# Router stage of a two-layer encoder step: logits inside the output products, one spread on VectorE, identity products in TensorE's pauses

## Chip, core and metric

One core of one Trainium2 chip runs the whole program. The metric is device microseconds per execution. Before the change three runs gave 1261.56, 1264.34 and 1266.49 us, median 1264.34 us.

## What is computed

One inference step of an encoder trunk with two layers, for 512 prompt rows and 64 sample rows of width 1024. The kernel pads them to 640 rows, five tiles of 128 (tile 4 holds the sample rows). Cut to what the change touches:

```
h = x @ w_in                                   # q, k, v, u, gv
mixed = concat(rms_norm(attention(q,k,v)), rms_norm(gelu(u) * (tril(W) @ LN(gelu(gv)) + b))) @ w_o
x = layer_norm(ALPHA * x + mixed, ln1_g, ln1_b)
scores = sigmoid(x @ w_router); sel = scores + router_bias          # 16 experts in 4 groups
best group by the sum of its two best sel; the two best experts inside it; weights normalised
y = sum over the chosen experts e of weight * ((silu(x @ wg[e]) * (x @ wu[e])) @ wd[e])
x = layer_norm(ALPHA * x + y, ln2_g, ln2_b)
```

## The kernel before

Each engine has its own instruction stream, written out by hand and held together by semaphores; an engine runs its stream strictly in the order written. A loop over the layers encloses everything, so each place in the code runs twice.

**Rounds.** After the projections, TensorE goes through rounds t = 0 to 7. A round may hold the attention scores of tile t, the output product of tile t-3 (`output`), the transposition and use of the attention weights of tile t-1 (`weighted_values`), the transposition of the normalised mixer outputs of tile t-2 (`turn_mixed`, tiles `mt`), the transposition of finished rows (`turn_rows_out`, tiles `rt`), and the router's logits of tile t-4 (`expert_logits`). An output product has two halves, c = 0 into PSUM bank A and c = 1 into bank B, each of 8 steps m = 0 to 7 of three 128x512 matmuls (`product`, L1608): 24 matmuls a half. The logits are computed from the rows before layer norm, with the gain folded into the router's weights, so that they need only the transposed rows `x1_t` that ScalarE copies out of PSUM (`router_rows_out`, L805); a correction with column sums (`sums`) follows on VectorE. One tile's logits are 8 source matmuls of 16 columns, which the trace shows as 16 instructions (L1744).

**VectorE** adds each output half to x (`mixed_out`, L1163), takes row statistics, subtracts the mean times the gain (`centre`, L1170; in halves for the last tile, L1365) and multiplies by the reciprocal deviation and adds the shift (`spread`, L1176). After round 7 it turns logits into scores for tiles 0 to 3, picks their experts, and does the same for tile 4 at the end, to `pick` at L1405. TensorE then counts ranks (L1795, L1798), VectorE makes the lists `cur_src` of the first experts' rows, and GpSimd gathers these rows from `x1_dram` (L617). GpSimd then sends ten slot scatters (L637), before it gathers the rows of expert 2.

**The last tile.** Its spread is divided before the change: ScalarE multiplies (L860), after VectorE's `centred`; GpSimd adds the shift (L594), stores the rows (L596) and clears the tile `rows` (L599), which gathers fill.

**Experts.** Each of the 16 experts' weights comes in units of 1 MB, loaded by SyncE into a ring `raw` of four. ScalarE makes the high part `w_hi` (L392), VectorE the low part `w_lo` (L398, `split_lo`), TensorE multiplies three products per pair (L1831, L1854). A unit's place in the ring is free for the next load when its low part is done.

Of the kernel before, what the change touches and what calls it, by code (L numbers as in the profile page):

```python
# [27 lines left out]
P = 128  # L28
# [4 lines left out]
NT = 5  # L33
# [89 lines left out]
def build(nc, x_prompt, x_sample, cache_k, cache_v, w_in, sinks, gm_ln_g, gm_ln_b, gm_ws, gm_bs,  # L123
# [5 lines left out]
    with ctx:  # L129
# [3 lines left out]
        def sem(name):  # L133
            return ctx.enter_context(nc.semaphore(name))
# [167 lines left out]
        ln1_t_in, gained_done, logit_done = sem("ln1_t_in"), sem("gained_done"), sem("logit_done")  # L302
        tables_done, centred, w12_done = sem("tables_done"), sem("centred"), sem("w12_done")
        spread_done = sem("spread_done")
        score_done, pick_done, slot_done = sem("score_done"), sem("pick_done"), sem("slot_done")
# [224 lines left out]
        def _(pool):  # L530
# [24 lines left out]
            with pool.Fori(0, DEPTH) as l:  # L555
# [34 lines left out]
                for t in range(NT):  # L590
                    if t == NT - 1:
                        hold(spread_done, l + 1)
                        xt = x[:, t, :].rearrange("p (a c) -> p a c", a=2)
                        pool.tensor_tensor(xt, xt, ln1_shift, ALU.add).then_inc(x1_ready, 1)  # L594
                    hold(x1_ready, NT * l + t + 1)
                    pool.dma_start(x1_dram[t * P:(t + 1) * P, :], x[:, t, :]).then_inc(x1_out, 16)  # L596
                    if t == NT - 1:

                        pool.memset(rows[:, :, :], 0.0).then_inc(rows_zero, 1)  # L599
                    if t == 0:  # L600
# [100 lines left out]
        def _(act):  # L701
# [24 lines left out]
            with act.Fori(0, DEPTH) as l:  # L726
# [131 lines left out]
                scores_of(2, NT - 1, NT)  # L858
                act.wait_ge(centred, l + 1)
                act.activation(x[:, NT - 1, :], x[:, NT - 1, :], ACT.Copy, scale=rs[:, NT - 1:NT]).then_inc(spread_done, 1)  # L860
                act.activation(warm[:, 5:6], eps, ACT.Silu)
# [142 lines left out]
        def _(dve):  # L1004
# [49 lines left out]
            with dve.Fori(0, DEPTH) as l:  # L1054
# [178 lines left out]
                for t in range(NT + 2):  # L1233
# [4 lines left out]
                    if t == 0:  # L1238
                        for r in range(NT):
                            gmlp_out(r)  # L1240
                    if t >= 4:
                        logits_out(t - 4)
                    if t == NT + 1:
                        sums_out()
                    if t >= 2:
                        rms_norm(t - 2)
                    if t >= 3:
                        mixed_out(t - 3)
                    if t == NT + 1:
                        mixed_lo(t - 2)  # L1250
                    if 3 <= t < NT + 1:
                        layer_norm(t - 3)
# [30 lines left out]
                dve.tensor_tensor(neg_mean[:, 0:NB], mv[:, 0:NB, 0], rs[:, 0:NB], ALU.mult)  # L1283
                dve.tensor_tensor(tiles(logits[:, 0:NC]), tiles(raw_logits[:, 0:NC]), over_experts(rs[:, 0:NB]), ALU.mult)
                dve.drain()
                dve.tensor_tensor(tiles(spread_cols), over_tiles(col_sums[:, 0:NE]), over_experts(neg_mean[:, 0:NB]), ALU.mult)
                dve.drain()
                dve.tensor_tensor(logits[:, 0:NC], logits[:, 0:NC], spread_cols, ALU.subtract)
                dve.drain()
                dve.tensor_tensor(tiles(logits[:, 0:NC]), tiles(logits[:, 0:NC]), over_tiles(col_sums[:, NE:2 * NE]),  # L1290
                                  ALU.add).then_inc(logit_done, 1)
# [89 lines left out]
                dve.sem_inc(logit_done, 1)  # L1381
                centre_half(1).then_inc(centred, 1)

# [203 lines left out]
        def _(pe):  # L1587
# [12 lines left out]
            def product(name, col, units, n, last=None, a_hi=xt_hi, a_lo=xt_lo, then=None):  # L1600
# [45 lines left out]
            with pe.Fori(0, DEPTH) as l:  # L1646
# [69 lines left out]

                def output(t, then=None):
                    wait_read(pe, ("mt", t, 1), l)
                    for c in range(2):
                        if t == 0:  # L1720
                            wait_unit(pe, l, 9 + 2 * c)
                        wait_free(pe, ("wo", c, t), l)
                        product(("wo", c, t), 0, [(2 * c % RB, 0), ((2 * c + 1) % RB, 4)], HALF,
                                last=True if t == NT - 1 else None, a_hi=mt_hi, a_lo=mt_lo, then=then if c else None)

# [6 lines left out]

                def expert_logits(t, halves=(0, 1)):
                    name = ("logit", t)
                    if t == 0:
                        pe.wait_ge(gained_done, l + 1)
                        pe.sem_inc(held_pe, 1)
                    for h in halves:
                        wait_read(pe, ("rt", t, h), l)
                        if h == 0:  # L1740
                            pe.sem_inc(held_pe, 1)
                            wait_free(pe, name, l)
                        for k in range(4 * h, 4 * h + 4):
                            ins = pe.matmul(bank_of(name)[:, 0:NE], x1_t[:, k, :], gained[:, k, :],  # L1744
                                            start=(k == 0), stop=(k == KT_N - 1))
                    if halves[-1]:
                        done(ins, name)

# [10 lines left out]
                for t in range(NT + 3):  # L1759
# [4 lines left out]
                    if t == 0:  # L1764
# [48 lines left out]
                for e in range(2):  # L1813
                    indices((e,))


# [170 lines left out]
```

## Time and profile before

| | |
|---|---|
| median of 3 runs | 1264.34 us |
| the profiled execution | 1264.73 us |
| its span, first to last instruction | 1263.1 us |
| TensorE matmuls busy | 1066.4 us, 84% of the span |
| VectorE busy | 906.0 us, 72% |
| ScalarE busy | 703.6 us, 56% |
| GpSimd busy | 235.1 us, 19% |
| mean granted TensorE clock | 0.921 of full speed |

The shares are means over stages with different limits. The chain of work that ended last, followed back from the end, tells which engine a stage waits for; the timeline of one engine shows in brackets how long it stood idle before an instruction and what released it; the windows give the granted clock of a stretch (1.00 is 2.4 GHz, 0.50 is 1.2 GHz). All times of rows are microseconds from the span's start.

### The profile page before, as it was taken

What the parts mean: (1) busy time and instruction counts of PE and PEld (TensorE: products, weight loads), DVE (VectorE), ACT (ScalarE), POOL (GpSimd) and SP (SyncE); (2) the same over time, 40 slices, a digit from 0 to 9 for tenths busy, and PEclk for the clock granted to TensorE, in tenths of its full rate; (3) what the DMA queues carried; (4) which work ended last, traced back from release to release, by engine and by line L of the source; (5) the groups of instructions that cost most, each with busy time, mean ns of one, the idle gap of its engine ahead of it and who ended that gap; (6) DMA issues with size and microseconds to landing.
All of it is one profiled execution on the core that took longest, in us unless ns stands there. A gap on an engine that the chain in (4) does not pass through costs nothing.

```text
span 1263.1 us, 16601 instructions
## 1 busy us (share of the span) xinstructions
PE 1066.4 (84%) x5364; PEld 886.8 (70%) x5364; DVE 906.0 (72%) x1138; ACT 703.6 (56%) x859; POOL 235.1 (19%) x174
## 2 busy tenths in 40 slices
PE   4999799958799999999289988989499999999920
PEld 3887588747677777877169867877377877777820
DVE  2573865379688888887677648645878888788838
ACT  2413674265577777776423247533567777677720
POOL 3000000028112223110321000000642122221003
PEclk9999889978899999999589987999699999999975
DMA  9423100028899999999714202000599999999851
GB/s 292 139 81 100 67 35 25 17 70 273 298 363 359 375 354 356 377 361 332 285 42 155 87 15 84 26 34 17 161 344 362 365 355 379 367 355 366 325 195 59
DMA packets 115748, 273.26 MB, mean 216 GB/s; under 512 B 10144, under 2 KB 13184, under 8 KB 114528
## 3 DMA queue, kind: packets, MB, share of 16 engines
q1 hardware_dynamic: 98608, 227.36, 51.0%
q0 software_dynamic: 14464, 33.01, 7.5%
q10 hardware_dynamic: 2608, 12.06, 2.6%
q8 instruction: 33, 0.54, 0.2%
q14 instruction: 35, 0.29, 0.1%
HBM read 262.02 MB, written 25.22 MB: 227 GB/s over the span
## 4 chain that ended last, share of the span: by engine, by line
PE 42%; DMA 19%; DVE 14%; issue 12%; ACT 7%; DVEq 2%; POOL 1%; POOLq 1%; ACTq 1%; SPq 0%
DMA raw<-in_w_gate 16%; PE bankA L1608 10%; PE bankB L1608 8%; DVE w_lo L398 6%; ACT w_hi L392 4%; PE bankC L1608 4%; PE bankD L1608 3%; PE bankA L1831 3%; DVE xt_lo L413 3%; PE bankG L1677 2%; PE bankB L1831 2%; PE bankC L1854 2%; PE bankD L1854 2%; PE bankE L1597 2%; PE bankH L1744 1%
## 5 line engine op out<-in xcount | busy, mean ns | idle before, releaser
L398 DVE TENSOR_TENSOR w_lo<-raw,w_hi 128x2048 fp32r<-128x2048 f32 x216 | 487.5, 2269 | 110.0 <-ACT w_hi L392 108.9
L392 ACT ACTIVATE w_hi<-raw 128x2048 fp32r<-128x2048 f32 x216 | 410.1, 1902 | 226.3 <-DMA raw<-in_w_down 57.0
L1831 PE MATMUL bankA<-w_hi,xt_hi 128*128 128x512 f32 x256 | 104.7, 409 | 25.3 <-DVE xt_lo L413 24.7
L1831 PE MATMUL bankB<-w_hi,xt_hi 128*128 128x512 f32 x256 | 102.8, 402 | 0.0
L1831 PE MATMUL bankA<-w_hi,xt_lo 128*128 128x512 f32 x256 | 102.0, 398 | 0.0
L1831 PE MATMUL bankA<-w_lo,xt_hi 128*128 128x512 f32 x256 | 101.7, 397 | 0.0
L1831 PE MATMUL bankB<-w_hi,xt_lo 128*128 128x512 f32 x256 | 100.2, 391 | 0.0
L1831 PE MATMUL bankB<-w_lo,xt_hi 128*128 128x512 f32 x256 | 99.8, 390 | 0.0
L623 POOL DMA_INDIRECT y_rows<-expert_out,idx x32 | 55.6, 1737 | 213.9 <-ACT expert_out L888 205.3
L617 POOL DMA_INDIRECT rows<-x_rows,idx x24 | 48.0, 2000 | 248.3 <-PE bankF L1597 232.4
L1831 PEld LDWEIGHTS bankA<-w_hi,xt_hi 128*128 128x128 f32 x256 | 49.4, 193 | 45.8 <-issue 36.1
L408 ACT ACTIVATE xt_hi<-bankE 128x512 fp32r<-128x512 f32 x42 | 24.5, 584 | 66.5 <-PE bankE L1597 66.4
L1831 PEld LDWEIGHTS bankA<-w_hi,xt_lo 128*128 128x128 f32 x256 | 49.2, 192 | 10.7
L1854 PE MATMUL bankC<-w_hi,xt_hi 128*128 128x512 f32 x128 | 53.6, 418 | 3.3 <-DVE xt_lo L413 3.3
L1831 PEld LDWEIGHTS bankA<-w_lo,xt_hi 128*128 128x128 f32 x256 | 49.4, 193 | 9.7
L1831 PEld LDWEIGHTS bankB<-w_hi,xt_lo 128*128 128x128 f32 x256 | 48.0, 188 | 10.5
L1831 PEld LDWEIGHTS bankB<-w_lo,xt_hi 128*128 128x128 f32 x256 | 48.2, 188 | 9.2
L1831 PEld LDWEIGHTS bankB<-w_hi,xt_hi 128*128 128x128 f32 x256 | 48.1, 188 | 9.0
L413 DVE TENSOR_TENSOR xt_lo<-bankE,xt_hi 128x512 fp32r<-128x512 f32 x42 | 28.7, 684 | 33.6 <-ACT xt_hi L408 33.6
L1854 PE MATMUL bankC<-w_hi,xt_lo 128*128 128x512 f32 x128 | 51.0, 398 | 0.0
L1854 PE MATMUL bankC<-w_lo,xt_hi 128*128 128x512 f32 x128 | 50.8, 397 | 0.0
L1854 PE MATMUL bankD<-w_hi,xt_hi 128*128 128x512 f32 x128 | 50.6, 395 | 0.0
(357 smaller groups left out, 2501.1 us busy)
## 6 DMA issues: line engine op xcount, KB each, us to landing
raw<-in_w_gate SPq DMA_DIRECT2D x64, 1024.0 KB, 8.2
raw<-in_w_up SPq DMA_DIRECT2D x64, 1024.0 KB, 7.9
raw<-in_w_down SPq DMA_DIRECT2D x64, 1024.0 KB, 7.3
raw<-in_w_in SPq DMA_DIRECT2D x12, 1024.0 KB, 9.8
raw<-in_w_o SPq DMA_DIRECT2D x8, 1024.0 KB, 5.4
y_rows<-y_rows ACTq DMA_DIRECT2D x8, 1024.0 KB, 7.9
x_rows<-x POOLq DMA_DIRECT2D x10, 512.0 KB, 3.0
raw<-in_w_in SPq DMA_DIRECT2D x4, 512.0 KB, 8.4
```

Of the source, the lines that this page charges most:

```text
L392: act.activation(w_hi[:, s % RB, :, 0:n], raw[:, s % RB, :, 0:n], ACT.Copy).then_inc(hi_done, 1)
L398: dve.tensor_tensor(w_lo[:, s % RB, :, 0:n], raw[:, s % RB, :, 0:n], w_hi[:, s % RB, :, 0:n].bitcast(F32), ALU.subtract).then_inc(lo_done, 1)
L408: act.activation(dst, bank_of(name)[:, :].rearrange("p (k n) -> p k n", k=4), ACT.Copy).then_inc(s, 1)
L413: read(dve.tensor_tensor(lo, bank_of(name)[:, :].rearrange("p (k n) -> p k n", k=4), hi.bitcast(F32), ALU.subtract), name)
L617: pool.indirect_dma_start(out=rows[:, e % 2, :], out_offset=None, in_=x1_dram, in_offset=bass.IndirectOffsetOnAxis(ap=src.bitcast(U32), ax ...
L623: pool.indirect_dma_start(out=y2_dram, out_offset=bass.IndirectOffsetOnAxis(ap=idx[:, e, 0:1].bitcast(U32), axis=0), in_=expert_out[:, e % ...
L1597: ins = pe.transpose(bank_of(name)[:, k * P:(k + 1) * P], src, ident)
L1608: ins = pe.matmul(out, a[:, k, col:col + P], w[:, slot, j, 0:n], start=(m == 0 and a is a_hi and w is w_hi), stop=(m == len(steps) - 1 and ...
L1677: ins = pe.matmul(bank_of(("o", t))[:, h * 64:(h + 1) * 64], probs_t[:, j % 2, 2 * a + b, :], v[b], start=(b == (0 if t else 1)), stop=(b ...
L1744: ins = pe.matmul(bank_of(name)[:, 0:NE], x1_t[:, k, :], gained[:, k, :], start=(k == 0), stop=(k == KT_N - 1))
L1831: ins = pe.matmul(out, a[:, 4 * k + t, (c % 2) * P:(c % 2 + 1) * P], w[:, (s + k) % RB, t, :], start=(k == t == 0 and a is xt_hi and w is ...
L1854: ins = pe.matmul(bank_of(f"down{h}")[:, :], a[:, 2 * j + r, cols], w[:, (s + j) % RB, 2 * r + h, :], start=(j == r == 0 and a is xt_hi an ...
```

## The change

Three things are changed, in both layers.

First, `output` runs before the logits in a round, and `product` calls a function after each step m. In rounds 4 to 7 `beside_first` places two of a tile's eight logit matmuls after each of the steps 0 to 3 of half A. In round 7 `beside_last` places the transposition of the last tile's first half after step 3 of half B, as before, and four of its logit matmuls after steps 6 and 7. The matmul for `sums` moves behind the output product of round 6. VectorE's copies of logits move behind `rms_norm`, and tile 3 is spread before its logits are read.

Second, the last tile is spread by one instruction on VectorE, right behind its second `centre_half`. ScalarE's multiplication and GpSimd's addition go, with the semaphores `centred` and `spread_done`. ScalarE clears `rows` in place of GpSimd, when that spread is done.

Third, TensorE multiplies the identity by itself into bank A, 14 times behind the last logits and 10 times behind the lists of the first two experts (`idle_products`); nothing reads these products.

```diff
@@ GpSimd
                 for t in range(NT):
-                    if t == NT - 1:
-                        hold(spread_done, l + 1)
-                        xt = x[:, t, :].rearrange("p (a c) -> p a c", a=2)
-                        pool.tensor_tensor(xt, xt, ln1_shift, ALU.add).then_inc(x1_ready, 1)
                     hold(x1_ready, NT * l + t + 1)
                     pool.dma_start(x1_dram[t * P:(t + 1) * P, :], x[:, t, :]).then_inc(x1_out, 16)
-                    if t == NT - 1:
-                        pool.memset(rows[:, :, :], 0.0).then_inc(rows_zero, 1)
@@ ScalarE
                 scores_of(2, NT - 1, NT)
-                act.wait_ge(centred, l + 1)
-                act.activation(x[:, NT - 1, :], x[:, NT - 1, :], ACT.Copy, scale=rs[:, NT - 1:NT]).then_inc(spread_done, 1)
+                act.wait_ge(x1_ready, NT * l + NT)
+                act.activation(rows.rearrange("p a (b n) -> p (a b) n", n=P), ident.unsqueeze(1).to_broadcast([P, 2 * KT_N, P]),
+                               ACT.Copy, scale=0.0).then_inc(rows_zero, 1)
@@ VectorE, rounds
+                    if t >= 2:
+                        rms_norm(t - 2)
                     if t >= 4:
                         logits_out(t - 4)
-                    if t == NT + 1:
-                        sums_out()
-                    if t >= 2:
-                        rms_norm(t - 2)
...
                         mixed_lo(t - 2)
+                        sums_out()
@@ VectorE, tile 3
                 row_stats(NB - 1).then_inc(var1_done, 1)
-                logits_out(NB - 1)
...
-                dve.reciprocal(rs[:, NB - 1:NB], sd[:, NB - 1:NB])
-                dve.drain()
+                spread(NB - 1, ln1_shift).then_inc(x1_ready, 1)
                 dve.tensor_tensor(neg_mean[:, 0:NB], mv[:, 0:NB, 0], rs[:, 0:NB], ALU.mult)
...
+                logits_out(NB - 1)
...
-                xt = x[:, NB - 1, :].rearrange("p (a c) -> p a c", a=2)
-                dve.scalar_tensor_tensor(out=xt, in0=xt, scalar=rs[:, NB - 1:NB], in1=ln1_shift,
-                                         op0=ALU.mult, op1=ALU.add).then_inc(x1_ready, 1)
@@ VectorE, tile 4
-                centre_half(1).then_inc(centred, 1)
+                centre_half(1)
+                xt = x[:, r, :].rearrange("p (a c) -> p a c", a=2)
+                dve.drain()
+                dve.scalar_tensor_tensor(out=xt, in0=xt, scalar=rs[:, r:NT], in1=ln1_shift,
+                                         op0=ALU.mult, op1=ALU.add).then_inc(x1_ready, 1)
@@ TensorE
-                    if then is not None and m == 3:
-                        then()
+                    if then is not None:
+                        then(m)
...
+                def beside_first(t):
+                    def then(m):
+                        if m < 4:
+                            expert_logits(t, (2 * m, 2 * m + 1))
+                    return then
+                def beside_last(m):
+                    if m == 3:
+                        turn_rows_out(NT - 1, (0,))
+                    if m >= 6:
+                        expert_logits(NT - 1, (2 * m - 12, 2 * m - 11))
...
-                    if t >= 4:
-                        expert_logits(t - 4)
+                    if t >= 3:
+                        output(t - 3, beside_first(t - 4) if t >= 4 else None, beside_last if t == NT + 2 else None)
                     if t == NT + 1:
...
-                    if t >= 3:
-                        output(t - 3, (lambda: turn_rows_out(NT - 1, (0,))) if t == NT + 2 else None)
...
-                expert_logits(NT - 1, (0,))
                 turn_rows_out(NT - 1, (1,))
-                expert_logits(NT - 1, (1,))
+                expert_logits(NT - 1, range(4, KT_N))
+                def idle_products(n):
+                    wait_free(pe, "gate", l)
+                    for _ in range(n):
+                        pe.matmul(bank_of("gate")[:, 0:P], ident, ident, start=True, stop=True)
+                idle_products(14)
...
                 for e in range(2):
                     indices((e,))
+                idle_products(10)
```

Three places in the order of the instructions. Round 5 on TensorE, before and after: `mt_hi` and `mt_lo` are the transposed mixer outputs, `ws,x_t` are the logits. The first two rows are the end of the round before.

```order
L1597 MATMUL bankF<-ident,u 128x128 x4
L337 REGISTER_ALU
L1744 MATMUL bankH<-ws,x_t 128x16 x8
L341 REGISTER_ALU
L1608 MATMUL bankA<-w_hi,mt_hi 128x512
L1608 MATMUL bankA<-w_lo,mt_hi 128x512
L1608 MATMUL bankA<-w_hi,mt_lo 128x512
```

```order
L1589 MATMUL bankF<-ident,u 128x128 x4
L340 REGISTER_ALU
L1600 MATMUL bankA<-w_hi,mt_hi 128x512
L1600 MATMUL bankA<-w_lo,mt_hi 128x512
L1600 MATMUL bankA<-w_hi,mt_lo 128x512
L336 REGISTER_ALU
L1736 MATMUL bankH<-ws,x_t 128x16 x2
```

The logits, which stood ahead of half A in a block of eight, now follow its first three matmuls in pairs.

The end of the router on VectorE, before and after: `sel` is the first use of tile 4's scores.

```order
L1378 SCALAR_TENSOR_TENSOR small<-bankH,small,ws 128x16
L1365 SCALAR_TENSOR_TENSOR x<-x,small,table 128x512
L1385 TENSOR_TENSOR sel<-score,small 128x16
L1310 TENSOR_TENSOR work_wide<-sel 128x4x2
L1311 TENSOR_TENSOR work_wide<-sel 128x4x2
```

```order
L1366 SCALAR_TENSOR_TENSOR small<-bankH,small,ws 128x16
L1353 SCALAR_TENSOR_TENSOR x<-x,small,table 128x512
L1373 SCALAR_TENSOR_TENSOR x<-x,small,ln_shift 128x1024
L1377 TENSOR_TENSOR sel<-score,small 128x16
L1298 TENSOR_TENSOR work_wide<-sel 128x4x2
```

One instruction of 128x1024, the spread of tile 4, now stands ahead of `sel`.

GpSimd at the last stores of rows, before and after:

```order
L596 DMA x_rows<-x 128x1024
L533 REGISTER_ALU
L594 TENSOR_TENSOR x<-x,ln_shift 128x1024
L596 DMA x_rows<-x 128x1024
L599 MEMSET rows 128x2048
L611 DMA table<-in_ln_g 128x1024
```

```order
L591 DMA x_rows<-x 128x1024 x2
L603 DMA table<-in_ln_g 128x1024
L604 DMA table<-in_ln_b 128x1024
L532 REGISTER_ALU x2
L532 ISA
L609 DMA rows<-x_rows,cur_src 128x1024
```

The addition and the clearing are gone from GpSimd's queue; nothing but DMA issues is left in it there.

## Rows read from the trace of the kernel before

**Rows 1.** Chain that ended last, first layer: start, us, what

```profile
189.42 1.89 PE bankH L1744 x16
191.31 5.60 PE bankA L1608 x24
...
212.74 7.14 PE bankA L1608 x24
...
219.88 5.44 PE bankB L1608 x24
...
236.61 7.17 PE bankA L1608 x24
```

**Rows 2.** Timeline of TensorE: start, us, engine, line, operation [idle before it <-releaser]

```profile
233.76 1.95 PE L1744 MATMUL bankH<-ws,x_t 128*128 128x16 f32 x16 [1.45 <-ACT x_t L805]
...
236.45 0.60 PE L1608 MATMUL bankA<-w_hi,mt_hi 128*128 128x512 f32 x1
...
263.25 0.60 PE L1597 MATMUL bankC<-ident,x 128*128 128x128 f32 x4
...
263.93 0.39 PE L1608 MATMUL bankB<-w_lo,mt_hi 128*128 128x512 f32 x1
```

**Rows 3.** Windows: us, busy PE, PEld, DVE, ACT, POOL, granted clock, DMA, GB/s

```profile
209.20:212.60 3.40, 1.95 (x19) 1.82 (x17) 1.29 (x2) 3.26 (x9) 0.00 (x0) 1.00 0.38 154
...
212.60:219.00 6.40, 6.40 (x23) 5.19 (x23) 1.66 (x4) 0.16 (x1) 0.00 (x0) 0.73 0.01 3
...
592.00:595.00 3.00, 1.35 (x9) 0.94 (x8) 2.50 (x4) 1.26 (x3) 0.61 (x1) 1.00 0.65 192
```

**Rows 4.** Timeline of VectorE, first layer, rounds 5 to 7

```profile
210.17 0.68 DVE L413 TENSOR_TENSOR mt_lo<-bankF,mt_hi 128x512 fp32r<-128x512 f32 x1
...
233.14 0.68 DVE L413 TENSOR_TENSOR mt_lo<-bankF,mt_hi 128x512 fp32r<-128x512 f32 x1
...
266.65 0.69 DVE L1163 SCALAR_TENSOR_TENSOR x<-x,bankB 128x512 f32<-128x512 f32 x1 [0.74 <-PE bankB L1608]
```

**Rows 5.** Timeline of VectorE, first layer, a spread and the router's end

```profile
256.37 1.28 DVE L1293 SCALAR_TENSOR_TENSOR x<-x,small,ln_shift 128x1024 f32<-128x1024 f32 x1
...
271.13 0.17 DVE L1385 TENSOR_TENSOR sel<-score,small 128x16 f32<-128x16 f32 x1
...
272.72 2.22 DVE L1396 TENSOR_TENSOR in_group<-sel,r 128x16 f32<-128x16 f32 x1
...
275.82 2.08 DVE L1405 TENSOR_SCALAR pick<-last,consts 128x16 bf16<-128x16 f32 x1
```

**Rows 6.** Timeline of GpSimd (POOL), first layer, the last tile

```profile
272.57 2.34 POOL L594 TENSOR_TENSOR x<-x,ln_shift 128x1024 f32<-128x1024 f32 x1 [13.82 <-ACT x L860]
...
276.05 1.82 POOL L599 MEMSET rows<- 128x2048 f32 x1
```

**Rows 7.** Timeline of TensorE, first layer, small work and waits

```profile
138.83 1.16 PE L1708 MATMUL bankG<-gv,ws_t 128*128 128x128 f32 x8
...
268.80 1.06 PE L1744 MATMUL bankH<-ws,x_t 128*128 128x16 f32 x8 [0.69 <-ACT x_t L805]
...
277.96 0.26 PE L1795 MATMUL bankH<-pick,before_b 128*128 128x96 bf16 x1 [8.10 <-DVE pick L1405]
...
322.75 1.12 PE L1597 MATMUL bankE<-ident,rows 128*128 128x128 f32 x4 [7.25 <-DMA rows<-x_rows,cur_src]
```

**Rows 8.** Timeline of ScalarE, first layer, the first expert's rows

```profile
286.87 0.60 ACT L408 ACTIVATE xt_hi<-bankE 128x512 fp32r<-128x512 f32 x1 [3.50 <-PE bankE L1597]
```

**Rows 9.** Timeline of GpSimd, the seventh slot scatter of either layer

```profile
301.58 3.09 POOL L637 DMA_INDIRECT slot_rows<-ints,slots  x1 [0.30 <-issue]
...
916.01 0.98 POOL L637 DMA_INDIRECT slot_rows<-ints,slots  x1 [0.30 <-issue]
```

**Rows 10.** Timelines of VectorE and TensorE, second layer, expert waits

```profile
912.19 0.17 DVE L1420 TENSOR_REDUCE first_idx<-bankG 128x2 f32<-128x8 f32 x1 [0.61 <-PE bankG L1809]
...
932.34 0.66 PE L1597 MATMUL bankE<-ident,rows 128*128 128x128 f32 x4 [2.40 <-DMA rows<-x_rows,cur_src]
```

More of the change, by code:

```diff
@@ L302, in build @@
         ln1_t_in, gained_done, logit_done = sem("ln1_t_in"), sem("gained_done"), sem("logit_done")
-        tables_done, centred, w12_done = sem("tables_done"), sem("centred"), sem("w12_done")
-        spread_done = sem("spread_done")
+        tables_done, w12_done = sem("tables_done"), sem("w12_done")
         score_done, pick_done, slot_done = sem("score_done"), sem("pick_done"), sem("slot_done")
@@ L1280, in _ @@
                 dve.wait_ge(sd1_done, NT * l + NB)
-                dve.reciprocal(rs[:, NB - 1:NB], sd[:, NB - 1:NB])
+                spread(NB - 1, ln1_shift).then_inc(x1_ready, 1)
+                dve.tensor_tensor(neg_mean[:, 0:NB], mv[:, 0:NB, 0], rs[:, 0:NB], ALU.mult)
                 dve.drain()
-                dve.tensor_tensor(neg_mean[:, 0:NB], mv[:, 0:NB, 0], rs[:, 0:NB], ALU.mult)
+                dve.tensor_tensor(tiles(spread_cols), over_tiles(col_sums[:, 0:NE]), over_experts(neg_mean[:, 0:NB]), ALU.mult)
+                logits_out(NB - 1)
+                dve.drain()
+                dve.tensor_tensor(tiles(spread_cols), over_tiles(col_sums[:, NE:2 * NE]), tiles(spread_cols), ALU.subtract)
                 dve.tensor_tensor(tiles(logits[:, 0:NC]), tiles(raw_logits[:, 0:NC]), over_experts(rs[:, 0:NB]), ALU.mult)
                 dve.drain()
-                dve.tensor_tensor(tiles(spread_cols), over_tiles(col_sums[:, 0:NE]), over_experts(neg_mean[:, 0:NB]), ALU.mult)
-                dve.drain()
[L1288 to L1291, printed above, removed]
-                xt = x[:, NB - 1, :].rearrange("p (a c) -> p a c", a=2)
-                dve.scalar_tensor_tensor(out=xt, in0=xt, scalar=rs[:, NB - 1:NB], in1=ln1_shift,
-                                         op0=ALU.mult, op1=ALU.add).then_inc(x1_ready, 1)
+                dve.tensor_tensor(logits[:, 0:NC], logits[:, 0:NC], spread_cols, ALU.add).then_inc(logit_done, 1)
                 dve.wait_ge(tables_done, l + 1)
@@ L1381, in _ @@
                 dve.sem_inc(logit_done, 1)
-                centre_half(1).then_inc(centred, 1)
+                centre_half(1)
+                xt = x[:, r, :].rearrange("p (a c) -> p a c", a=2)
+                dve.drain()
+                dve.scalar_tensor_tensor(out=xt, in0=xt, scalar=rs[:, r:NT], in1=ln1_shift,
+                                         op0=ALU.mult, op1=ALU.add).then_inc(x1_ready, 1)
                 dve.wait_ge(score_done, 2 * l + 2)
@@ L1715, in turn_mixed, with output @@
                         turn(("mt", t, h), l, [v[:, t, k * P:(k + 1) * P] for k in range(4)])
-                def output(t, then=None):
+                def output(t, first=None, second=None):
                     wait_read(pe, ("mt", t, 1), l)
@@ L1723, in output @@
                         product(("wo", c, t), 0, [(2 * c % RB, 0), ((2 * c + 1) % RB, 4)], HALF,
-                                last=True if t == NT - 1 else None, a_hi=mt_hi, a_lo=mt_lo, then=then if c else None)
+                                last=True if t == NT - 1 else None, a_hi=mt_hi, a_lo=mt_lo, then=(first, second)[c])
                 def turn_rows_out(t, halves=(0, 1)):
@@ L1731, in turn_rows_out, with expert_logits @@
                         turn(("rt", t, h), l, [x[:, t, (4 * h + k) * P:(4 * h + k + 1) * P] for k in range(4)])
-                def expert_logits(t, halves=(0, 1)):
+                def expert_logits(t, ks):
                     name = ("logit", t)
[L1735 to L1740, printed above, removed]
+                    for k in ks:
+                        if k == 0:
+                            wait_read(pe, ("rt", t, 0), l)
                             pe.sem_inc(held_pe, 1)
                             wait_free(pe, name, l)
[L1743 to L1747, printed above, removed]
+                            pe.sem_inc(held_pe, 1)
+                            pe.wait_ge(gained_done, l + 1)
+                        if k == 4:
+                            wait_read(pe, ("rt", t, 1), l)
+                        ins = pe.matmul(bank_of(name)[:, 0:NE], x1_t[:, k, :], gained[:, k, :],
+                                        start=(k == 0), stop=(k == KT_N - 1))
+                        if k == KT_N - 1:
+                            done(ins, name)
+                def beside_first(t):
[8 more added lines that the diff above has]
+                        expert_logits(NT - 1, (2 * m - 12, 2 * m - 11))
                 pe.wait_ge(k_done, NT * (l + 1))
```

## Prediction

> **What bounds the kernel now.** I read first the chain of work that ended last. In the rounds it stays on TensorE [rows 1]: for each tile 16 logit matmuls, 24 products of half A, 24 of half B. The reader is to see that half A lasts 5.60 us in round 4 and 7.14 and 7.17 in rounds 5 and 6, for the same 24 products, while half B lasts 5.44. The first layer's rows are shown; the second's stand 614.5 us later, with the same lengths to a few hundredths where I speak of both.
>
> Next TensorE's timeline [rows 2] and the granted clock [rows 3]. In rounds 5 to 7 TensorE stands idle (1.45 us in round 6) for ScalarE's `x_t`, runs the logits, and only then begins half A. The clock is still 1.00 over that idle time and the logits, and 0.73 over the first 6.4 us of half A: about half of that stretch ran at 1.2 GHz. At 592.0, an idle time of 1.65 us of 3.0, with no logits behind it, leaves the clock at 1.00. So what precedes the fall is the idle time and the block of 16-column matmuls together, and idle time of that length alone does not bring it.
>
> Then VectorE. After half B of the last tile it is VectorE's chain, from 266.65 to `pick` at 277.9, that everything waits for: TensorE stands idle 8.10 us before the rank at 277.96 [rows 4, 7]. In that chain two instructions of 128x16 last 2.22 and 2.08 us, where their like lasts 0.17 [rows 5]. Each stands beside a GpSimd instruction and ends with it: the addition, 272.57 to 274.91, and the clearing, 276.05 to 277.87 [rows 6]. So I read both as VectorE shut out by GpSimd, 2.05 and 1.91 us a layer.
>
> Behind the rank TensorE waits 7.25 us for expert 2's rows in the first layer and 2.40 in the second [rows 7, 10]; from there the experts follow the weights' DMA.
>
> **The sum, by layer.** It is made against the profiled execution, 1264.73 us (a span of 1263.1 and 1.6 around it), which is 0.4 above the median of the runs.
>
> *Round 4, nothing.* No idle time and no low clock there: 1.89 of logits and 5.60 of half A before, the same matmuls mixed after.
>
> *Round 5, 1.24.* Half A needs `mt_lo`, whose last piece ends at 210.85 [rows 4]; it can start 0.15 later, and the chain counts a product 0.15 behind its start. From 211.15: half A at the full clock 5.60, the logits inside it 1.89, half B 5.44, end at 224.08. Before, it ended at 212.74 + 7.14 + 5.44 = 225.32 [rows 1]. The logits' own price inside half A no row shows. The nearest is the block of four transpositions inside half B: 0.68 from its start to the second product behind it, less one product's 0.23, is 0.45 [rows 2], 0.11 for each instruction, so no surcharge for the interruption. Four pairs are 16 instructions; at 0.45 for four that is 1.80, and I take 1.89. Bounds: 1.4, if each group's first weight load hides under a long product (one of four free), and 2.4, if the change of shape costs 0.15 a group. That is +0.5 or -0.5 a round.
>
> *Round 6, 1.93.* `mt_lo` ends at 233.82, half A counts from 234.12, and 5.60 + 1.89 + 5.44 and 0.24 for `sums`, now behind the product, end at 247.29; before, 236.61 + 7.17 + 5.44 = 249.22 [rows 1, 4].
>
> *Round 7, 0.1.* TensorE could gain here as in round 5, but VectorE, which adds half B, stood idle for it only 0.74 us [rows 4], and its row of work becomes longer ahead of that point by some 0.6, as tile 3's spread (1.28 in all, [rows 5]) now stands ahead of its logits. So VectorE becomes the bound: 0.74 less 0.6. Bounds 0.7 and -0.3.
>
> *The tail, 2.68.* The addition's and the clearing's locks go, 2.05 + 1.91; the spread comes onto VectorE's chain ahead of `sel`, 1.28 [rows 5]. ScalarE's clearing waits for that spread and is hidden if it ends before the first expert's rows are split: ScalarE has 3.50 us idle ahead of that [rows 8], and it loses a multiplication; the clearing by GpSimd took 1.82 [rows 6]. GpSimd's gathers wait for it, and stay behind VectorE's lists in any case. I price it at nothing, with 0.2 as the upper bound.
>
> The Trainium skill, "SBUF — State Buffer", section "SBUF: two separate sides", says that VectorE and GpSimd share a port pair under an exclusive lock, in which the loser is blocked wholly, and that VectorE with two SBUF inputs takes it only against a GpSimd operation that reads SBUF. The addition agrees with this. A clearing reads nothing, and L1405 has one tensor as input, so by the page it would be blocked only in a two-port mode; by the other reading the tail would gain 1.91 less.
>
> *The identity products, nothing on the path.* Eight f32 matmuls of 128 columns took 1.16 [rows 7]. The 28 behind the last logits (each product being two instructions) cost 4.1 us at the full clock and 8.1 at the low one; the logits end at 269.86, and the rank, moved up by 2.68, comes at 275.28: room 5.4. The 20 behind the lists cost 2.9 or 5.8; the room to the first rows is about 4.3. They are covered at the full clock, which half B leaves behind. What they can give: the first expert's products at the full clock. Yet TensorE there waits for GpSimd's gather in the first layer (7.25), so a quicker product buys only a longer wait; in the second VectorE waits 0.61 for TensorE behind it [rows 10], of which I count half, 0.3.
>
> Per layer 1.24 + 1.93 + 0.1 + 2.68 = 5.95, both 11.9, and 0.3: 12.2. 1264.73 - 12.2 = 1252.5, and 0.4 lower for the median: **1252.1**. The bounds of the logits' price (2 rounds, 2 layers, 0.5 each) and of round 7 give 1249 to 1255.
>
> **The rivals.**
>
> *The slot scatters, both ways.* GpSimd's ten slot scatters stand ahead of the gather of expert 2. The seventh took 3.09 us in the first layer and 0.98 in the second [rows 9], and so TensorE's wait is 7.25 or 2.40: a difference of 4.85 a layer. The router now comes some 6 us earlier against weight splits that follow a DMA stream, so either layer can fall either way. Both short: 1252.1 - 4.85 = 1247.2. Both long: 1256.9.
>
> The Trainium skill, same page and section, says that a VectorE operation in such a mode holds up the descriptors which GpSimd writes for its own DMAs. By that rule a scatter would be long beside a weight split and short without one; [rows 9] show that both lengths occur, and the time that each would give is the two figures above.
>
> *The clock falls all the same.* If the idle time alone brought it, halves A of rounds 5 to 7 would stay at about 7.15: 1.54 and 1.57 lost in rounds 5 and 6, and up to 1.3 in round 7, 4.4 a layer: 1252.1 + 8.8 = 1260.9. Against it stands the row at 592.0 [rows 3].
>
> *Slower.* The small matmuls, now spread over halves A of four rounds and the end of half B in round 7, keep the clock low in the products among which they stand. One product takes 0.43 at the low clock and 0.23 at the full one, so each costs 0.2; the change's 5.95 are eaten by 30 more low products in a layer. If 48 more ran low in each layer, 12 in each of the four rounds: 1252.1 + 19.2 = 1271.3. For it: the clock fell behind such matmuls. Against it: round 4, where 16 of them came without idle time, stayed at 5.60 [rows 1].
>
> *The identity products hold up the rank.* At the low clock they end at 277.96, 2.7 behind the earlier `pick`: 5.4 in both layers, 1257.5. Against it: half B leaves the full clock.
>
> *The locks are none.* If the clearing is not what stretches L1405, the tail gains 1.91 less: 1255.9; if neither is, 1252.1 + 7.9 = 1260.0. The ends that coincide in [rows 5] and [rows 6] speak against it.
>
> **How the numbers follow.** Forecast 0.55; scatters both short 0.14, both long 0.11; clock falls all the same 0.09; identity products late 0.05; locks are none 0.03; slower 0.03. The predicted time is the likeliest case's, 1252.1. The range, 1246.0 to 1259.5, takes in both scatter cases with a margin, the late identity products and the bounds of the unknown prices. What this kernel's measurement can tell from no change is 0.5%: below 1258.0 or above 1270.7. Faster: 0.55 + 0.14 + 0.11 and what of the last cases lies below 1258.0, 0.83. Slower 0.03. Within: 0.14, most of it the clock.
>
> **What would show it.** In the timeline of TensorE, halves A of rounds 5 and 6 should start some 1.6 and 2.5 us earlier against the `mt_lo` before them and last 7.5 us with the logits in them, with the granted clock at 1.00. On VectorE no instruction of 128x16 at L1396 and L1405 of before should last over 0.3; from the end of the last half B to `pick` should be some 2.7 shorter. TensorE's wait before expert 2's rows should be 7 and 2 us. Wrong it is, if the granted clock in rounds 4 to 7 is below 0.95, if the rank waits for an identity product, if L1405's like still lasts 2 us, or if the scatters take another pattern, which moves the time by 4.85 and shows in that wait alone.

## The result, and the profile after

Four runs of the changed kernel gave 1242.93 to 1251.14 us, median **1247.89**, beside 1265.41 for four runs of before: a ratio of 0.986 with a 95% interval of 0.982 to 0.991. Two longer comparisons on two chips, of twelve and of eleven runs (c1 and c3 below), gave 0.994 (0.991 to 0.997) and 0.9945 (0.991 to 0.998), that is 1254.4 against 1261.6 and 1254.0 against 1260.0. One execution of c3 (1866.5 us) and one of e9 (2186.0 us) lie far outside all others and are left out. The change makes the kernel faster, by some 0.5 to 1.4%. How much it gives is better read from the stages than from the first four runs.

The table measures each stretch on TensorE, in every layer of the traces at hand, us. A round is counted from the end of a half B to the end of the next.

| stretch | before, 2 traces | changed, 3 traces |
|---|---|---|
| round 5 | 22.97 22.99 21.39 23.01 | 24.77 24.79 26.41 23.19 26.35 21.60 |
| round 6 | 23.91 23.86 23.90 23.90 | 21.61 21.61 21.60 21.64 21.62 21.62 |
| round 7 | 17.38 17.36 17.37 17.37 | 16.60 16.60 16.60 16.63 16.60 16.60 |
| last half B to `pick` | 11.29 11.26 11.30 11.27 | 9.53 8.90 8.93 8.92 8.90 8.89 |
| rank to the start of the experts' last product | 322.3 318.1 321.1 313.6 | 315.4 315.9 319.1 319.1 317.4 319.0 |

From round 3's half B to the rank the mean is 97.8 before and 94.5 after: 3.3 us a layer, 6.6 in all. The experts' stretch (the last row) differs by 1.1 us between the two means, and by up to 8.7 within a column.

The chain that ended last, first layer of the changed kernel, rounds 5 and 6 (start, us, what; L1600 is a product, L1736 the logits):

```profile
209.33 0.96 PE bankA L1600 x3
210.29 0.35 PE bankH L1736 x4
...
212.19 1.47 PE bankA L1600 x3
213.66 0.67 PE bankH L1736 x4
...
234.10 0.95 PE bankA L1600 x3
235.06 0.35 PE bankH L1736 x4
...
237.70 0.79 PE bankA L1600 x3
238.49 0.35 PE bankH L1736 x4
```

Three products and a pair of logits take 0.79 + 0.35 in round 6 and 1.47 + 0.67 in round 5: twice as long, for the same work. The windows (us, busy PE, PEld, DVE, ACT, POOL, granted clock, DMA, GB/s) give the reason:

```profile
211.50:216.50 5.00, 5.00 (x20) 4.42 (x19) 1.37 (x3) 0.00 (x0) 0.00 (x0) 0.50 0.02 3
...
234.00:241.70 7.70, 7.60 (x41) 6.56 (x42) 1.80 (x5) 1.82 (x6) 0.00 (x0) 1.00 0.01 2
```

The clock is 0.50 in round 5, that is 1.2 GHz, and 1.00 in round 6. Half A of round 5, which ran 7.14 before without logits [rows 1], lasts 10.76 with them.

VectorE's timeline at the end of the first layer's router answers to [rows 5]:

```profile
269.18 1.28 DVE L1373 SCALAR_TENSOR_TENSOR x<-x,small,ln_shift 128x1024 f32<-128x1024 f32 x1
270.38 0.17 DVE L1377 TENSOR_TENSOR sel<-score,small 128x16 f32<-128x16 f32 x1
...
271.98 0.18 DVE L1388 TENSOR_TENSOR in_group<-sel,r 128x16 f32<-128x16 f32 x1
...
273.05 0.23 DVE L1397 TENSOR_SCALAR pick<-last,consts 128x16 bf16<-128x16 f32 x1
```

The two instructions that lasted 2.22 and 2.08 now last 0.18 and 0.23, and the spread stands ahead of them. TensorE's timeline around the identity products, first and second layer (idle time and its end in brackets), answers to [rows 7]:

```profile
266.07 1.89 PE L1736 MATMUL bankH<-ws,x_t 128*128 128x16 f32 x8 [0.69 <-ACT x_t L797]
267.79 5.67 PE L1797 MATMUL bankA<-ident 128*128 128x128 f32 x28
273.34 0.22 PE L1806 MATMUL bankH<-pick,before_b 128*128 128x96 bf16 x1
...
873.66 1.07 PE L1736 MATMUL bankH<-ws,x_t 128*128 128x16 f32 x8 [0.69 <-ACT x_t L797]
874.58 3.37 PE L1797 MATMUL bankA<-ident 128*128 128x128 f32 x28
880.30 0.26 PE L1806 MATMUL bankH<-pick,before_b 128*128 128x96 bf16 x1 [2.35 <-DVE pick L1397]
```

In the first layer the last logits ran at a granted clock of 0.50 and the 28 instructions at 0.57, and these end as `pick` does (273.28); in the second there are 2.35 us to spare. Waits for expert 2's rows were 4.73 and 5.82 us, where [rows 7, 10] have 7.25 and 2.40:

```profile
314.84 1.12 PE L1589 MATMUL bankE<-ident,rows 128*128 128x128 f32 x4 [4.73 <-DMA rows<-x_rows,cur_src]
...
922.84 1.11 PE L1589 MATMUL bankE<-ident,rows 128*128 128x128 f32 x4 [5.82 <-DMA rows<-x_rows,cur_src]
```

### The profile page after: what moved, and what is told of

Same layout as the page of the kernel before. It is cut to its first block, busy times and chain, and to the rows that moved or that the text cites. A ratio compares the mean times of both kernels' runs of the same rounds, so it can differ in the third digit from the quotient of the medians.

```text
span 1248.6 us, 16799 instructions
## 1 busy us (share of the span) xinstructions
PE 1069.0 (86%) x5460; PEld 892.1 (71%) x5460; DVE 901.2 (72%) x1140; ACT 706.8 (57%) x859; POOL 214.5 (17%) x170
## 4 chain that ended last, share of the span: by engine, by line
PE 44%; DMA 16%; DVE 13%; issue 13%; ACT 6%; DVEq 3%; POOL 3%; POOLq 1%; ACTq 0%; SPq 0%
DMA raw<-in_w_gate 12%; PE bankA L1600 9%; PE bankB L1600 7%; DVE w_lo L397 4%; PE bankC L1600 4%; PE bankA L1843 4%; PE bankB L1843 4%; PE bankD L1600 4%; ACT w_hi L391 3%; DVE xt_lo L412 2%; POOL slot_rows L629 2%; PE bankC L1866 2%; PE bankG L1669 2%; PE bankD L1866 2%; PE bankE L1589 2%
## 5 line engine op out<-in xcount | busy, mean ns | idle before, releaser
L615 POOL DMA_INDIRECT y_rows<-expert_out,idx x32 | 50.1, 1566 | 215.3 <-ACT expert_out L882 215.3
L609 POOL DMA_INDIRECT rows<-x_rows,idx x24 | 40.8, 1699 | 249.9 <-PE bankF L1589 232.9
L1600 PE MATMUL bankA<-w_hi,mt_hi 128*128 128x512 f32 x80 | 38.7, 483 | 14.2 <-DVE mt_lo L412 7.7
```

Of the source, the lines that this page charges most:

```text
L609: pool.indirect_dma_start(out=rows[:, e % 2, :], out_offset=None, in_=x1_dram, in_offset=bass.IndirectOffsetOnAxis(ap=src.bitcast(U32), ax ...
L615: pool.indirect_dma_start(out=y2_dram, out_offset=bass.IndirectOffsetOnAxis(ap=idx[:, e, 0:1].bitcast(U32), axis=0), in_=expert_out[:, e % ...
```

## The experiments

Ratios are against runs of before on the same chip, with 95% intervals. "To the rank" is the stretch from round 3's half B to the rank in the two layers of the trace: 98.2 and 98.1 before, 95.2 and 94.6 in the changed kernel's first trace. Of these runs, e1 to e4 ran on one chip, c1, c2, e5 and e6 on a second, e8 to e10 on a third and c3 on a fourth, so e1 to e4 are compared with c1 by their ratios.

**Both kernels again (c1, c2, c3).** No edit.

> The changed kernel as it is, on the chip of this call, as the yardstick for the others and for a second trace. Theory (the change is worth what the steps of the trace add up to, and round 5 keeps the low clock in most executions): from the end of round 3's half B to the rank 94.5 to 95.3 us in a layer whose round 5 falls to the low clock and 91.4 in one that does not, against 98.2 before; tail from the last half B to pick 8.9; time 1248 to 1252 where before has 1262 to 1265. Rival (half of the first trace's gain lay in the experts, 272 us from expert 2's rows to the last products where before had 276 and 277, and comes from the change): 272 again in both layers.

> The kernel before as it is, for a second trace. Theory (the length of the experts varies by execution, by DMA): from expert 2's rows to the last products below 275 in at least one layer; all steps up to the rank as in the first trace within 0.2 us, 98.1 to 98.3 from round 3's half B to the rank. Rival (before's experts are longer by themselves): 275.5 or more in both layers.

> The changed kernel a third time, since its first two comparisons with before differ (0.986 and 0.994). Theory (the change is worth its steps up to the rank, 6 to 8 us, and the experts' length varies by execution): ratio 0.992 to 0.996; from round 3's half B to the rank 93 to 96.5 us by how round 5 falls; from the rank to the last down product anywhere from 313 to 322. Rival (the first comparison is the rule): ratio 0.985 to 0.988, and 315 to 316 from the rank to the last down product in both layers.

c1: 1254.36, ratio 0.994 (0.991 to 0.997). c3: 1253.99, 0.9945 (0.991 to 0.998). c2, one run of before: 1255.4. The stages are in the table above. To the rank c1 took 96.2 and 93.1, c3 96.2 and 91.4. c1's theory allowed 94.5 to 95.3 or 91.4 and missed in both layers, since round 5 has more lengths than two; its time of 1248 to 1252 missed as well. From the first `down` product, right behind expert 2's rows, to the last product before had 275.9 and 277.2 in its first trace and 274.4 and 270.7 in c2; the changed kernel 272.3 and 271.7, then 277.8 and 278.6 in c1, 271.8 and 278.7 in c3. So the length of the experts belongs to the execution, and the rival falls. Of the 14.46 us between the first two traces' spans, 6.5 lay ahead of the ranks, 9.1 in the experts, and the rest took 1.2 back. The wait for expert 2's rows also varies, in the same code (c1, then c3, both layers):

```profile
315.80 1.12 PE L1589 MATMUL bankE<-ident,rows 128*128 128x128 f32 x4 [2.86 <-DMA rows<-x_rows,cur_src]
...
920.98 0.66 PE L1589 MATMUL bankE<-ident,rows 128*128 128x128 f32 x4 [1.92 <-DMA rows<-x_rows,cur_src]
```

```profile
318.21 1.11 PE L1589 MATMUL bankE<-ident,rows 128*128 128x128 f32 x4 [7.15 <-DMA rows<-x_rows,cur_src]
...
916.00 0.66 PE L1589 MATMUL bankE<-ident,rows 128*128 128x128 f32 x4 [2.63 <-DMA rows<-x_rows,cur_src]
```

The traces also tell which scatters are long. In VectorE's timeline of before, these are the weight splits at the two scatters of [rows 9], first and second layer:

```profile
301.54 2.28 DVE L398 TENSOR_TENSOR w_lo<-raw,w_hi 128x2048 fp32r<-128x2048 f32 x1
...
916.04 2.30 DVE L398 TENSOR_TENSOR w_lo<-raw,w_hi 128x2048 fp32r<-128x2048 f32 x1
```

The scatter of 3.09 us begins at 301.58, just inside a split, and ends at 304.67, 0.86 behind the split's end. The scatter of 0.98 us begins at 916.01, just ahead of one. Of the 280 scatters of all 14 traces, 215 begin inside a split and end 0.85 to 0.92 us behind its end; the other 65 begin outside one, or within its first 0.04 us, and last 0.98 to 1.15. So a scatter's length depends on where it falls against VectorE's splits. No run moves a split to test this.

c2 missed one point: one of its four halves A of rounds 5 and 6, round 5 in the first layer, lasted 5.55 us and not 7.14, behind the same idle time and the same block of logits; that layer took 96.6 to the rank.

**Identity products ahead of half A (e4, e9).** e4 fills the wait for `mt_lo` in rounds 5 to 7; e9 uses `{5: 6}` alone.

```diff
+                    if t in {5: 6, 6: 6, 7: 2}:
+                        wait_free(pe, ("wo", 0, t - 3), l)
+                        for _ in range({5: 6, 6: 6, 7: 2}[t]):
+                            pe.matmul(bank["A"][:, 0:P], ident, ident, start=True, stop=True)
                     if t >= 3:
                         output(t - 3, ...)
```

> The changed kernel with identity products also ahead of half A in rounds 5 (6 products), 6 (6) and 7 (2), while TensorE waits for mt_lo. Theory (the idle time of 1.57 us ahead of round 5's half A is what brings the clock down there): round 5's half A with the logits lasts 7.5 us instead of 10.76, at a granted clock of 1.00; 3.2 us a layer, time 1241.5. Rival (the 16-column logits between the products bring it down, the idle time does not matter): round 5 stays at 10.5 to 10.8, time 1248.

> The changed kernel with identity products ahead of half A in round 5 alone; rounds 6 and 7 keep their idle time. Theory (the fall in round 5 is what spares rounds 6 and 7): round 5 takes 21.6, and one of rounds 6 and 7 falls in its place, 1.6 to 3.2 us longer; time 1252 to 1255. Rival (rounds 6 and 7 stay at the full clock by themselves, as they did in the one layer in which round 5 did not fall): 21.6, 21.6 and 16.6, time 1248.

e4: 1247.77, ratio 0.989 (0.984 to 0.994). Both layers take 91.4 to 91.5 to the rank, 3.0 less than the changed kernel's mean, 6 us in all, and round 5 takes 21.59 and 21.63. The time alone settles less: the ratio's interval overlaps the changed kernel's (0.991 to 0.997), and 1247.77 is the rival's number, as the theory's 1241.5 was counted from the first four runs. TensorE's timeline and the window of round 5 in e4's first layer:

```profile
209.34 1.50 PE L1780 MATMUL bankA<-ident 128*128 128x128 f32 x12
211.07 0.50 PE L1600 MATMUL bankA<-w_hi,mt_hi 128*128 128x512 f32 x1 [0.23 <-DVE mt_lo L412]
```

```profile
209.20:221.50 12.30, 12.07 (x69) 10.34 (x68) 3.88 (x8) 3.59 (x9) 0.00 (x0) 1.00 0.11 44
```

The idle time of 1.57 us is 0.23, half A comes no later, and the clock stays at 1.00. e9: 1246.8, ratio 0.991 (0.988 to 0.994), with 21.6, 21.6 and 16.6 in both layers: rounds 6 and 7 keep the full clock with their idle time, and the first expectation (the fall only moves) missed. The interleaved kernel without fill was traced in 14 layers (three traces of it, and e1, e3, e5, e6): round 5 took 21.6 in two of them and 23.2 to 26.4 in twelve. With fill it took 21.6 in six of six (e4, e9, e8).

**The logits in a block (e2, e10).** e2 puts the block back; e10 is e2 with five identity products ahead of the block in rounds 5 to 7.

```diff
+                    if t >= 4:
+                        expert_logits(t - 4, range(KT_N))
                     if t >= 3:
-                        output(t - 3, beside_first(t - 4) if t >= 4 else None, beside_last ...)
+                        output(t - 3, None, beside_last ...)
...
-                    if m >= 6:
-                        expert_logits(NT - 1, (2 * m - 12, 2 * m - 11))
...
+                expert_logits(NT - 1, range(0, 4))
```

> The changed kernel with the logits again in one block ahead of half A, and the last tile's first four behind half B; the tail and the identity products as changed. Theory from the changed kernel's trace (interleaving lost 1.8 us in round 5, whose half A ran 10.76 us with the logits in it, at the low clock, and won 2.3 in round 6 and 0.6 up to the last half B): round 5 from the end of one half B to the next 23.0 instead of 24.8, round 6 23.9 instead of 21.6, the last half B 0.6 later; 1.1 us a layer, time 1250. Rival (interleaving is worth the 3.3 us a layer of my sum): 1254.5.

> The kernel with the logits in one block ahead of half A (run before without fill), with 5 identity products in the idle time ahead of that block in rounds 5 to 7. Theory (the idle time brings the clock down, the block of 16-column matmuls does not): halves A of rounds 5 to 7 last 5.6 instead of 7.15, 81.8 us from round 3's half B to the last one instead of 86.6, time 1246. Rival (the block of small matmuls is enough, as my prediction had it): 86.6, time 1255.

e2: 1255.27, ratio 0.996 (0.992 to 1.000); 95.4 and 95.5 to the rank, rounds 5, 6 and 7 at 23.1, 23.1 and 17.8 to 17.9. Interleaving, as the change has it, is worth about 1 us a layer (95.4 less the changed kernel's mean of 94.5), as the theory had it; the time fell on the rival's 1254.5, but the changed kernel itself took 1254 in c1 and c3. e10: 1250.94, ratio 0.9946 (0.991 to 0.998); 94.3 and 91.1. The expected 1246 was missed, by the first layer: there halves A of rounds 4 and 6 fell, each to a granted clock of 0.77. Its chain, first layer:

```profile
189.21 1.89 PE bankH L1736 x16
191.10 7.21 PE bankA L1600 x24
...
212.30 1.93 PE bankH L1736 x16
214.23 5.58 PE bankA L1600 x24
...
233.82 1.93 PE bankH L1736 x16
235.75 7.18 PE bankA L1600 x24
```

Round 6 had 0.45 us of idle time left ahead of its block, and round 4 has none in any kernel here. With the whole idle time ahead of the block, 6 of 6 halves A of rounds 5 to 7 fell in e2 and 11 of 12 in before; with most of it filled, 1 of 6 in e10; in round 4, without idle time, 1 of 8 (before, c2, e2, e10). So the idle time ahead of the block brings the fall nearly always; the block without it was followed by a fall once. The idle time brings it without the block too (round 5 of the changed kernel, by e4); with neither idle time nor block round 5 never fell, in six layers.

**The tail (e3, e6).** e3 gives the last tile's spread back to ScalarE and GpSimd and the clearing back to GpSimd; e6 gives back the clearing alone. Shown is e6's addition on GpSimd; its clearing on ScalarE goes.

```diff
                     pool.dma_start(x1_dram[t * P:(t + 1) * P, :], x[:, t, :]).then_inc(x1_out, 16)
+                    if t == NT - 1:
+                        pool.memset(rows[:, :, :], 0.0).then_inc(rows_zero, 1)
```

> The changed kernel with the last tile's spread again divided (ScalarE multiplies, GpSimd adds) and the tile rows cleared by GpSimd; logits and identity products as changed. Theory (GpSimd shuts VectorE out): two short VectorE instructions of the router's end last 2 us again, pick comes 1.9 to 2.7 us later after the last half B in each layer, time 1252 to 1253. Rival (what is late after the last tile is then TensorE or the gathers, and the locks were hidden): 1248.

> The changed kernel with only the clearing of the tile rows given back to GpSimd, behind its store of the last tile; the spread stays on VectorE. Theory (a clearing of 1.82 us shuts VectorE out although it reads nothing): one short VectorE instruction between the spread and pick lasts 1.5 to 2.1 us, and from the last half B to pick it is 10.4 to 10.9 us instead of 8.9; time 3 to 4 above the changed kernel's. Rival (a clearing reads nothing and does not block an instruction with one input): no instruction over 0.3, 8.9, and the same time.

e3: 1258.19, ratio 0.997 (0.994 to 1.000), 97.2 and 97.8 to the rank, 11.45 and 12.07 from the last half B to `pick`. e6: 1251.71, ratio 0.995 (0.991 to 0.998), 11.05 and 10.41. In the first layer of e3, VectorE and then GpSimd:

```profile
271.76 2.23 DVE L1389 TENSOR_TENSOR in_group<-sel,r 128x16 f32<-128x16 f32 x1
...
274.87 2.08 DVE L1398 TENSOR_SCALAR pick<-last,consts 128x16 bf16<-128x16 f32 x1
```

```profile
271.61 2.34 POOL L594 TENSOR_TENSOR x<-x,ln_shift 128x1024 f32<-128x1024 f32 x1 [14.64 <-ACT x L859]
...
275.09 1.82 POOL L598 MEMSET rows<- 128x2048 f32 x1
```

And in the first layer of e6:

```profile
273.33 1.67 DVE L1384 TENSOR_SCALAR r<-last 128x4 f32<-128x4 f32 x1
```

```profile
273.15 1.82 POOL L593 MEMSET rows<- 128x2048 f32 x1
```

In e6 the clearing comes earlier than in before, and another instruction, of 128x4, waits it out: 1.67 us, in the second layer too. It is GpSimd's instruction that does this, not the place in the router. In e3 `pick` begins 0.22 us ahead of the clearing, and yet it ends with it. The time of e6 does not show the loss: the expected 3 to 4 us more did not come, and its median lies 2.7 us below c1's. In the traced run the experts were short (272.4 and 273.1 from the first `down` product); of the other runs no trace tells. So the verdict is the trace's. In e3 the tail is 2.5 and 3.2 us longer than in c1, and the time of 1258.19 lies above the expected 1252 to 1253.

**Without identity products (e1).**

```diff
-                idle_products(14)
+                idle_products(0)
...
-                idle_products(10)
+                idle_products(0)
```

> The changed kernel without any identity product. Theory (they cost and give next to nothing on the path): the rank comes 0.2 us earlier in the first layer, where the trace of the changed kernel shows it right behind the 28 identity instructions (end 273.46, pick 273.28), and at the same place in the second; the first expert's 24 products run wholly at the low clock, 8.3 us instead of 7.2, which only lengthens the time ahead of the lists of experts 2 and 3 by 1.1; TensorE's wait for expert 2's rows stays with the slot scatters. Time 1248, within 2 us of the changed kernel's 1247.9. Rival (what the change gave beyond my 12.2 us comes from the clock that these products keep up): 1251 to 1253.

1254.45, ratio 0.993 (0.990 to 0.997), as c1 and c3, where the changed kernel also missed the 1248 that was expected here. From the last half B to `pick` 8.90 in both layers; from the first expert's first product to the first of the next 24 it took 8.2 and 9.2 us, in the changed kernel 8.3 and 6.7. In the second layer the identity products raise the clock there, and the ratios show no gain from it.

**The gathers ahead (e5), and with the fill (e8).** GpSimd sends the gathers of experts 2 and 3 behind the fourth slot scatter.

```diff
                         .then_inc(slots_out, 16)
-                hold(cur_done, 3 * l + 3)
-                for e in range(2, ON_CHIP):
-                    hold(filled["F"], nth(("xe", 1), l, 0, e - 2))
-                    gather(e, cur_src[:, e:e + 1])
+                    if c == 3:
+                        hold(cur_done, 3 * l + 3)
+                        for e in range(2, ON_CHIP):
+                            hold(filled["F"], nth(("xe", 1), l, 0, e - 2))
+                            gather(e, cur_src[:, e:e + 1])
```

> The changed kernel with the gathers of experts 2 and 3 sent by GpSimd ahead of the last six slot scatters. Theory (the scatters set when expert 2's rows arrive, and TensorE's wait of 4.7 and 5.8 us for them holds up the weights' stream): the wait falls to under 1 us, from the rank to the first down product 38 to 39 us instead of 43 to 44, time 8 to 10 us below the changed kernel's. Rival (the weights' DMA bounds that stretch anyway): the wait moves behind, to w_hi's waits for DMA, and the time is within 2 us.

> The changed kernel with both additions that gained: identity products ahead of half A in rounds 5 to 7, and the gathers of experts 2 and 3 ahead of the last six slot scatters. Theory (they act in different places and add up: 6.6 and 4.5 us below the changed kernel's 1254.4 on this chip): 91.4 from round 3's half B to the rank, no wait of TensorE for expert 2's rows, 1243. Rival (a quicker front only meets the weights' DMA sooner): 1248, as with the fill alone.

e5: 1249.86, ratio 0.990 (0.986 to 0.994), 4.5 us below c1 on the same chip, half of what was expected; the two intervals overlap. TensorE no longer waits for these rows, but for their low part two instructions later (first layer):

```profile
311.84 0.60 PE L1589 MATMUL bankE<-ident,rows 128*128 128x128 f32 x4
312.27 0.60 PE L1589 MATMUL bankF<-ident,rows 128*128 128x128 f32 x4
315.86 0.49 PE L1866 MATMUL bankC<-w_hi,xt_hi 128*128 128x512 f32 x1 [2.98 <-DVE xt_lo L412]
```

So from the rank to the first `down` product it took 40.7 and 40.8, not the expected 38 to 39; c1 has 41.3 and 40.5, and 43 to 46 stand where a wait was long. e8: **1241.57**, ratio 0.989 (0.984 to 0.993), 91.6 and 91.4 to the rank; 5.2 us below e9 on the same chip. It is the fastest kernel here. That the two additions add up is not shown: e4 and e5 ran on other chips, and their ratios (0.989 and 0.990) lie within e8's interval.

## Why the prediction was right, and which steps failed

Forecast were 1252.1 and a gain of 12.2, likeliest faster; measured were 1247.9, then 1254.4 and 1254.0. Direction and range hold in all three. The sum of the steps does not: it had 5.95 a layer ahead of the experts, and 3.3 came. One of the prediction's own signs of being wrong came (the scatters took another pattern: waits of 4.73 and 5.82 us, not 7 and 2), and another in part: the granted clock over rounds 4 to 7 was 0.96 in the first trace and 0.94 in the first layers of c1 and c3, where 0.95 was the bound.

- **Round 4, nothing:** 22.61 became 22.66. Right, so the pairs cost no surcharge at the full clock.
- **Round 5, 1.24: failed.** It lost 1.9 on the mean. The step that failed is the reading of [rows 3], that idle time of this length alone does not bring the clock down. The idle time of that row follows products of 128x512, which run up to 592.9, and four transpositions; round 5's follows 7 us of transpositions and 64-column matmuls. e4 and e9 (round 5 alone) filled the idle time and changed nothing else, and the fall went with it, 3.2 us in a layer at the size of the first trace. My rival of the clock supposed falls in rounds 5 to 7 at the old size; the fall came in round 5 alone, and there it also stretched the logits. The traces tell that round 5 needed the fill; why round 6, with the same 1.57 us of idle time behind the same kind of work, never did in 14 layers is open. Round 7 waits 0.70.
- **Round 6, 1.93:** 2.27. Right, with the full clock as forecast.
- **Round 7, 0.1:** 0.77, above the bound of 0.7. Mis-sized: VectorE's row of work ahead of half B grew by 0.1 and not by 0.6. From one addition of half B to the next it took 17.38 before, 0.74 of it idle, and 16.75 now, with no idle time left at its end.
- **The tail, 2.68:** 2.36 where the logits run at the full clock, 1.76 where the last logits took 1.89 us instead of 1.07. Right, if 0.3 to 0.9 short; e3 shows both locks and e6 that of the clearing alone. On the Trainium skill's "SBUF — State Buffer", section "SBUF: two separate sides": of an instruction with one SBUF input the page says that it contends with GpSimd only in a two-port mode. Two instructions with one tensor as input ended with the clearing here, after 2.08 us in e3 (`pick`, which also takes a scalar per partition) and 1.67 in e6; whether they run in that mode no run shows.
- **The identity products, nothing:** right by e1, as far as its interval tells. In the first layer they ended with `pick`, as the rival at the low clock would have it, and cost nothing.
- **The scatters:** the rival's mechanism is there in both directions (waits from 1.92 to 7.15 in one and the same kernel), its price is not. In before, the layers with waits over 7 us took 322.3 and 321.1 from the rank to the last product, the others 318.1 and 313.6. In the changed kernel the three longest waits (4.73, 5.82, 7.15) stand with 315.4 to 317.4, the three short ones with 319.0 and 319.1: what the wait cost, the experts behind it gave back. What decides between the two is open. e5 took the whole wait away, and 4.5 us came, over both layers. The cited rule on GpSimd's descriptors speaks of two-port modes; a weight split reads two tensors, and no run shows that it runs in such a mode. The rows bear out the long scatter beside a split, not that reason for it.

With the fall in round 5 filled, e4, e9 and e8 come to 91.4 to 91.6 to the rank, 6.7 us a layer below before's first trace: the sum's 5.95 and round 7's excess of 0.7. That the forecast time fits is luck in part: the long comparisons gained 7.2 and 6.0 us, some half of the forecast 12.2, and the first one 17.5, in whose traces 9.1 of 14.46 us is the experts' own spread. The range was wide enough for both.

## What to carry to other kernels

Idle time of TensorE behind short work can be worth filling even where it is 1.6 us and nothing seems to wait for it: in round 5 it cost not the wait but the half speed of the products behind it. In rounds 6 and 7 filling it gave nothing (e4 against e9), so try it place by place. Read a gain in the stage where the edit acts, in several layers and traces, before believing a total: here the two spans differed by 14.46 us, and 9.1 of it was the experts' own spread. A short VectorE instruction that lasts 2 us is read best beside GpSimd's timeline, and a long scatter of GpSimd beside VectorE's.

## What the runs showed of the hardware

The granted clock fell in the same code at the same place in some executions and not in others: round 5 of the changed kernel took 21.6, 23.2, 24.8 or 26.4 us in 14 layers, with nothing in between, and half A of before 5.55 once where it else took 7.1 to 7.2. Beside a GpSimd clearing of 128x2048 (1.82 us) VectorE instructions of 128x4 and 128x16 lasted 1.67 and 2.08 us, which else last 0.17 and 0.23. A scatter that GpSimd issued inside a VectorE weight split of 2.3 us ended 0.85 to 0.92 us behind the split (215 of 215), others took 0.98 to 1.15, so ten of them took anything from 22.0 to 27.3 us in before and the changed kernel. The stretch of the experts varied by 8.7 us between layers of the same kernel, 313.6 to 322.3.
